# The second half of the weights two blocks ahead is split in the following block

## The reference

```python
def _layer(x, xc, mod, mod_c, rope, need_ctx, p):          # first block, layers 0 and 1
    h = _modulate(_rms_norm(x, p['g_pre_mix']), sh1, sc1)
    ua, us, um = _split_in(h @ p['w_in'])
    y_att = _blocked_attention(q, k, v)                    # 4 heads
    y_sc  = _short_conv(us, p['sc_conv_w'])
    y_ssd = _ssd_output(y_scan, xs, z, ...)                # two-way state space scan, 8 heads
    y = jnp.concatenate([y_att, y_sc, y_ssd], axis=-1) @ p['w_out']
    x = x + g1 * _rms_norm(y, p['g_post_mix'])
    f = jnp.square(jax.nn.relu(h2 @ p['w_ff1'])) @ p['w_ff2']      # D_FF = 4096
    return x + g2 * _rms_norm(f, p['g_post_ffn']), ...

def second_block(x, p, ...):
    for i in range(2):
        # i = 0: mixer A, i = 1: mixer B
        x = layer_norm(DEEPNORM_ALPHA * x + mixer(x), ln_g[i], ln_b[i])
        gate = jax.nn.sigmoid(x @ ple_w_gate[i])
        x = x + gate * (p[i] @ ple_w_proj[i])

def mixer_a(x, w_in, w_out, cos, sin):    # 3 groups of dilated windows, 16 heads of 64
    ...                                   # q and k with rope, banded softmax, merge, * silu(z), @ w_out
def mixer_b(x, w_in, sinks, w_out, cos, sin):   # window of 128, 16 q heads on 2 kv heads, sinks
```

## Time and profile before

| | before |
|---|---|
| device time, three runs | 1848.59, 1841.23, 1852.05 us (median 1848.59) |
| the profiled execution | 1843.46 us, span 1841.3 us |
| mean granted TensorE clock | 0.917 |
| TensorE busy | 1601.3 us, 87% |
| VectorE busy | 1027.6 us, 56% |
| ScalarE busy | 895.2 us, 49% |
| chain that ended last | TensorE 67%, VectorE 13%, ScalarE 12%, issue 4%, DMA 2% |
| DMA | 225.41 MB, mean 122 GB/s |

### The profile page before, as it was taken

How to read it: one execution, slowest core, us unless ns; L and a number is a source line. 1 busy time by engine, 2 the same in 40 slices (tenths; PEclk the granted TensorE clock), 3 DMA queues, 4 the chain that set the end, 5 groups by cost and what they waited for, 6 DMA issues and landing times.

```text
span 1841.3 us, 25909 instructions
## 1 busy us (share of the span) xinstructions
PE 1601.3 (87%) x10291; PEld 1350.9 (73%) x10291; DVE 1027.6 (56%) x1754; ACT 895.2 (49%) x1470; POOL 105.3 (6%) x114
## 2 busy tenths in 40 slices
PE   6899878859999999779896799997999978887687
PEld 3577556637888888647664699997989977786577
DVE  1563546666343434575636766667676664565555
ACT  4353545434232313245545454455676665456646
POOL 3100014020000000020003100000000000000000
PEclk8799978888999999979987899998999989988899
DMA  9422445402422232212356345554544433242221
GB/s 295 135 65 73 160 157 169 129 26 70 134 94 92 91 109 94 79 35 80 115 161 206 115 137 184 184 195 150 165 155 144 141 111 104 81 138 92 92 88 51
DMA packets 221561, 225.41 MB, mean 122 GB/s; under 512 B 6154, under 2 KB 219984, under 8 KB 221392
## 3 DMA queue, kind: packets, MB, share of 16 engines
q1 hardware_dynamic: 220736, 223.63, 37.8%
q0 software_dynamic: 704, 0.12, 0.0%
HBM read 222.68 MB, written 1.05 MB: 122 GB/s over the span
## 4 chain that ended last, share of the span: by engine, by line
PE 67%; DVE 13%; ACT 12%; issue 4%; DMA 2%; SPq 0%; POOL 0%; DVEq 0%; ACTq 0%; POOLq 0%
PE bank L833 18%; PE bank L835 18%; PE bank L834 18%; ACT whi L1301 3%; ACT SH L1434 2%; PE bank L858 1%; PE bank L1065 1%; DVE AP L2324 1%; DVE wlo L1809 1%; DVE XT L2099 1%; ACT AP L1672 1%; DMA raw<-in_w_mod_dram 1%; PE bank L847 1%; PE bank L1108 1%; PE bank L1163 1%
## 5 line engine op out<-in xcount | busy, mean ns | idle before, releaser
L1809 DVE TENSOR_TENSOR wlo<-raw,whi 128x1024 fp32r<-128x1024 f32 (+3 forms) x322 | 385.7, 1208 | 380.0 <-ACT whi L1301 376.6
L1301 ACT ACTIVATE whi<-raw 128x1024 fp32r<-128x1024 f32 (+3 forms) x322 | 333.2, 1045 | 411.4 <-PE bank L835 385.2
L833 PE MATMUL bank<-HH,whi 128*128 128x512 f32 (+3 forms) x656 | 254.5, 388 | 34.8 <-DVE HL L1831 29.5
L834 PE MATMUL bank<-HL,whi 128*128 128x512 f32 (+3 forms) x656 | 250.9, 382 | 0.0
L835 PE MATMUL bank<-HH,wlo 128*128 128x512 f32 (+3 forms) x656 | 250.7, 382 | 0.0
L833 PE MATMUL bank<-HA,whi 128*128 128x256 f32 x576 | 166.0, 288 | 11.2 <-DVE LA L1831 6.9
L833 PEld LDWEIGHTS bank<-HH,whi 128*128 128x128 f32 (+2 forms) x656 | 123.4, 188 | 68.9 <-issue 23.9
L834 PE MATMUL bank<-LA,whi 128*128 128x256 f32 x576 | 163.0, 283 | 0.0
L835 PE MATMUL bank<-HA,wlo 128*128 128x256 f32 x576 | 162.9, 283 | 0.0
L835 PEld LDWEIGHTS bank<-HH,wlo 128*128 128x128 f32 (+2 forms) x656 | 123.7, 189 | 26.9 <-issue 1.5
L834 PEld LDWEIGHTS bank<-HL,whi 128*128 128x128 f32 (+2 forms) x656 | 123.9, 189 | 25.9 <-issue 2.0
(11 more groups left out here) (352 smaller groups left out, 3316.9 us busy)
## 6 DMA issues: line engine op xcount, KB each, us to landing
raw<-in_w_ff_dram SPq DMA_DIRECT2D x64, 1024.0 KB, 5.3
raw<-in_w_mod_dram SPq DMA_DIRECT2D x48, 1024.0 KB, 5.2
raw<-in_a_w_in_dram SPq DMA_DIRECT2D x40, 1024.0 KB, 5.1
raw<-in_w_in_dram SPq DMA_DIRECT2D x16, 1024.0 KB, 5.2
raw<-in_b_w_in_dram SPq DMA_DIRECT2D x9, 1024.0 KB, 5.3
raw<-in_w_out_dram SPq DMA_DIRECT2D x8, 1024.0 KB, 5.2
raw<-in_ple_w_gate_dram SPq DMA_DIRECT2D x8, 1024.0 KB, 5.1
raw<-in_a_w_out_dram SPq DMA_DIRECT2D x4, 1024.0 KB, 5.4
```

The lines of the kernel that those rows point to most:

```text
L833: nc.tensor.matmul(o, wh, xh, start=start, stop=False, skip_group_check=shared)
L834: nc.tensor.matmul(o, wh, xl, start=False, stop=False, skip_group_check=shared)
L1301: f(whi[h % HALF_SLOTS][:, 0:n], raw[u.id % RAW_SLOTS][:, (h % 2) * n:(h % 2) * n + n], ACT.Copy)\
L1809: v.tensor_tensor(wlo[h % HALF_SLOTS][:, 0:n], raw[u.id % RAW_SLOTS][:, (h % 2) * n:(h % 2) * n + n], whi[h % HALF_SLOTS][:, 0:n].bitcast( ...
```

## The change

`halves_ahead` no longer counts two halves of block u + 2 for a packed block, but one, as for the others. So the second half of u + 2 is not split in block u, between `run_late()` and the emptying of the bank. It is the first thing in block u + 1, by `splits(u.halves_next)`, ahead of `run_late()`, on ScalarE and on VectorE. The steps that stand between the blocks u and u + 1 come before it. Packing, the three banks, the one bank for each block, and the numbers of slots are as they were.

```diff
@@ -642,7 +642,7 @@
         u.sid = n
     for u in units:
         u.halves_next = 2 * sum(v.id <= u.id + 1 for v in split_units) - 1
-        u.halves_ahead = u.halves_next + (2 if u.packed else 1) * sum(v.id == u.id + 2 for v in split_units)
+        u.halves_ahead = u.halves_next + sum(v.id == u.id + 2 for v in split_units)
     N_HALF = 2 * len(split_units)
```

## The result

| | before | after |
|---|---|---|
| device time, median of 20 runs | 1847.82 us (1838.55 to 1852.05) | 1854.78 us (1846.01 to 1863.78) |
| the profiled execution's span | 1841.3 us | 1852.0 us |
| mean granted TensorE clock | 0.917 | 0.909 |

The ratio is 1.0048, with a 95% interval of 1.0030 to 1.0067: the change makes the kernel about 0.5% slower, some 7 to 9 us. The forecast was 1850.1 us, 1.5 us above before, in a range of 1839 to 1862, with 73% on a difference within 0.5%. The time lies in the range. The difference is within 0.5% by a hair, and its interval reaches to both sides of 0.5%. The sum under the forecast was made of terms that were wrong on both sides and happened to cancel: that the time came out near is luck. Most of this part is about that.

What follows compares the result with a forecast made beforehand. No engine full; a chain exp, scale, transposes and scores, max sets the time. Stages -7.3, mixer B +5.75, mixer A +1.6, clock +1.4: +1.5 us, profiled 1845.0; the median lies 5.1 above, so 1850.1, range 1839 to 1862.

Steps and rivals of the forecast that it cites:

- Ends of stages: Sooner emptying: end of ff2 -2.3 us, w_out -2.4, ff1 to ff2 -1.9, two layer norms -0.3 each; sum -7.3.
- Mixer B: Scale behind the left-over split comes 2.35 us later, delaying max and the last turn; sum +5.75 us.
- E: In the attentions, the end of the exps of a pair; later steps are timed from it.
- the clock term: Mixer B: longer TensorE idle may put turn and scores of three blocks at the lower clock; 0 to +3.6, taken +1.4 us.
- the first aq block: Start of mixer B, no exp ahead: rope and TensorE's 5.78 us wait for roped queries shrink by 1.1 us.
- Mixer A: Max 1.35 us sooner, scale 2.35 later; pairs 0 to 3 +0.2, whole mixer taken as +1.6 us.
- What is queued behind: Behind VectorE's new wait stand scale and turn; weight reloads stay hidden with 3.5 us over; z0 0, at worst +2.
- a TensorE wait for wlo in mixer A: Sign named beforehand: TensorE waiting for low parts of split weights in mixer A would show the forecast wrong.
- (a): Rival: emptying is worth its wait at roped queries (-4.4) and mixer A turns (-10.8), with the 7.3: -22 us, 1826; 9%.
- (b): Rival: only gains of the stages count, later scale hidden everywhere, waits for AP not longer: -7.3 us, 1841.3; 13%.
- (c): Rival: later scale keeps TensorE at the lower clock through mixer B, making it the bound: 1870; 11%.
- (d): Rival: weight loads come late by some 1 us in ten blocks of mixer A: 1860; 4%.

Runs made afterwards that it cites:

- the second profile of before: The unchanged kernel before, run once more for a second profile: 1850.68 us in one run.
- Keeping eight blocks: Against before, change except eight mixer A blocks ahead of second max and exp: ratio 0.9954 with block 198 also kept, 0.9898 with VectorE scaling first in mixers and out2.
- the two experiments that part them: Against before: mixer blocks keep two halves, all others count one, 1834.06 us (0.9925); only mixer blocks count one, 1870.38 us (1.0130).

## Why the forecast came out as it did

- **Ends of stages: right in kind, small in size.** At the end of ff2 the YM addition starts 0.3 us after the matmuls and the wait for ACC is 2.42 us, as forecast (2.4). The four joints from ff1 to ff2 gave 0.6 to 0.7 us each, -2.5 in place of the -1.9 read off the waits of 0.4 to 0.5: a wait of TensorE is counted from the modelled end of a matmul, while the distance from start to start fell from 0.7 or 0.8 to 0.1. What the row of the feed-forward has beyond these two (-5.6 for -4.8) is within what the pace of its matmuls scatters. Each layer norm gave -0.9, not -0.3.
- **Mixer B: right in its steps, but for the end.** The first az block of the change:

```profile
1676.84 2.15 ACT L1301 ACTIVATE whi<-raw 128x1024 fp32r<-128x1024 f32 x2
...
1678.00 1.23 DVE L1809 TENSOR_TENSOR wlo<-raw,whi 128x1024 fp32r<-128x1024 f32 x1 [5.31 <-ACT whi L1301]
...
1679.67 1.01 DVE L2355 TENSOR_SCALAR AP<-AP,small 128x128 f32<-128x128 f32 x4
...
1680.74 1.54 PE L1163 MATMUL bank<-ident_sb,AP 128*128 128x128 f32 x6 [3.27 <-DVE AP L2355]
1682.21 1.66 PE L1138 MATMUL bank<-AK,AQ 64*128 64x128 f32 x8
...
1684.02 0.29 DVE L2324 CUSTOM_DVE_ANT_0 AP<-bank,mask_b_sb 128x128 f32<-128x128 f32 x1 [2.08 <-PE bank L1138]
```

  With E = 1676.81 the transposes start at E + 3.93 (forecast 3.92). Max is at E + 7.2 and not E + 5.75, because turn and scores ran at the lower level of the clock after 3.27 us of idle time (1.54 and 1.66 us in place of the 0.87 and 0.93 of the earlier trace rows): this is the clock term, taken as +1.4 for the whole mixer. The rope of the second aq block is at E + 5.2 (forecast 5.1). Against the first scores, the scores of the three later aq blocks are 3.5, 5.3 and 5.5 us later than before; the steps of the forecast with the clock term add up to 3.7, 5.4 and 5.9. Between there and the last turn 2.6 us are won back, which the forecast hasn't; the second profile of before is 2.0 us shorter there than the first, so most of this can be scatter. The last turn then adds 2.65 (forecast 2.35). The stretch is +7.6 for a forecast of 6.85 + 1.4, in which 6.85 is 5.75 without the -1.1 of the first aq block, which has its own row.
- **Mixer A: wrong, +10.1 for +1.6.** Two steps of the forecast failed. The first is the one under "What is queued behind", which asked only what stands behind VectorE's wait for the left-over whi. It didn't ask whether the left-over half itself is still in time. For that the position of TensorE has to be set against that of the other two engines, and here it is more than a block ahead. The text named "a TensorE wait for wlo in mixer A" as the sign of being wrong, and that sign appeared. With it pairs 0 to 3 lose 5.4 us for a forecast of +0.2. The second is the sum for pairs 4 to 7, +4.7 for some +1.4: counted from the product of pair 3, the turns of pairs 4, 5 and 6 are 1.1, 3.2 and 3.6 us later (forecast 1.1, 2.3 and 2.7), the 1.1 that was to be won back behind pair 6 isn't, and the last turn and product take another 1.0. Keeping eight blocks took most of both away. How the 10.1 us part between the half, the scale and the clock behind each wait no run here tells alone: none changes all of mixer A with the scale first.
- **First out2 blocks: missed, +3.9 and +3.7.** The list of what `run_late()` holds had the scale in it, but not the low part of the last pair, which TensorE waits for there.
- **Gates: missed, -7.3 with the first aq block (forecast -1.1).** The waits of TensorE before had a line for it, 3.6 us for the sigmoid, once; the prediction took only the ends of stages that it knew from the order of the code, and left the join from the gates to mixer B out. Parted, the first aq block gave -0.9, near its -1.1, and the gates -6.9, for which the forecast had nothing. About half of that is the wait, the rest is matmuls that no longer run at the lower level behind it. The Trainium skill, "TensorE: Matmul & The Clock Gate" (Part 1: The HAM clock gate), says that the clock falls after TensorE was idle; the rule was weighed in the prediction only against the change, while at the gates, as the traces show, it works for it.
- **The rivals.** (a) fell: the emptying isn't worth its wait in the mixers. (b) fell: the waits for AP grew. (c) did not come about: the blocks between two turns still get back to the upper level, and the mean clock of mixer B is 0.82, as in the earlier trace rows (from the first scores on it is 0.79, before 0.81). (d) was not seen: ScalarE's waits for raw weights are 19.8 us after and 20.4 before, none of them in the mixers.

The error of the parts was +8.5 us (mixer A) and +7.6 (out2) on one side and -6.2 (gates) and -2.5 (ends of stages) on the other. Only their sum was small, and that is luck: the two experiments that part them missed the prediction's sums by 4 us or more (-11.8 for -7.3) and by over 15 (+24.5 for +7 to +9).

## What to carry to other kernels

When a step is moved down a queue, ask three things of each place that it passes: who is behind it now, whether its own product is still in time for an engine that may be a block ahead, and in whose waiting time it had been hidden. Where stages differ, decide the order by stage: here the same one-line rule makes the kernel 12 us or more faster outside the mixers and 24 slower in them, and choosing by kind of block makes it 1.0% faster where the whole makes it 0.5% slower. Go through all waits of the bounding engine in the profile, those that occur once too; the dearest one here stood between two stages and cost twice its length.

## What the hardware showed

- A wait of 3.60 us of TensorE made the 50 or so short matmuls behind it twice as slow, and without the wait they weren't (0.42 and 0.28 us each, starts 0.21 and 0.11 us apart). Behind the 3.3 us of the second profile of before some 30 of them were slow. In mixer B the first turn took 1.54 us behind 2.79 to 3.75 us of idle time (four profiles), and 0.87 or 0.88 behind 0.68 to 1.28 (four profiles). The wait of 2.73 to 2.75 us at the first out2 block of mixer B comes between matmuls 0.12 us apart. In three of four profiles some 14 to 17 matmuls start 0.21 us apart, from 1.2 to 1.5 us behind it on, and the stretch is at +4.0 to +4.5; in the fourth none do, and it is at +2.3. So the same wait has cost its own length or nearly twice that.
- The feed-forward's matmuls follow each other 0.113 or 0.118 us apart, for tens of microseconds at a time, both at a granted clock of 1.00. Of fourteen profiles nine have the shorter distance nearly throughout, one the longer, four both. In that one, the slower pace took back the whole gain of the stretch. Its cause stays open.
- Two executions of the same instructions, 0 to 783 us, differed by up to 11 us (-2.9 to +8.3 against the first profile). A single pair of spans (10.7 us apart here) would have said little on a change of 7.
